# Sparse attention stage of a two-block kernel: values between the turns, masks by pairs, four logit banks, copies by head, gating on GpSimd

## The chip, the cores and the metric

One core of one Trainium2 chip runs the whole kernel. The metric is device time in microseconds (us); lower is better. All times are of one execution of the program.

## What is computed

The kernel computes two transformer-like blocks over 1024 tokens of width 1024. The change lies in the first one's attention. Eight heads of 64 share two key/value heads; each query attends to its causal keys, restricted to the 256 with the highest index score:

```python
logits = einsum('btkgd,btjkd->btkgj', q, k) * 64 ** -0.5
logits = where(selected, logits, -inf)          # causal, top 256 of the index scores
p = softmax(logits, axis=-1)
y_b = einsum('btkgj,btjkd->btkgd', p, v)
merged = concat([rms_norm(y_a, g_out_sgu), rms_norm(y_b, g_out_attn)])
```

y_a is the spatial gating's result, 512 features by 1024 tokens, which is normed in the same stage. merged then goes into the output projection and the rest of the network.

## The kernel before

`attend` is one block of instructions for each engine, between two barriers. Queries are taken in tiles of 128, in the order b = 1, 7, 6, 5, 4, 3, 2, 0; tile b sees b + 1 blocks of 128 keys. A step i is one head u of one tile, 64 steps in all; two steps make a pair p. Tiles with b of 4 and more are called wide here (over 512 keys, two PSUM banks for a head's logits), the others narrow (one bank). Everything is float32.

A step's life: TensorE multiplies queries and keys (`logits`, L1328; two heads of a pair side by side on halves of the rows). VectorE's `mask` (L1494) reads the logits from PSUM and the mask from SBUF, and writes masked logits and their extreme to SBUF. ScalarE's `exponentials` (L1418) works in place. TensorE turns the result with one transpose per block of keys (`turn`, L1342) into PSUM banks 2 and 3; a copy (VectorE L1542, ScalarE L1451) brings each bank to SBUF. After a tile's eight heads, TensorE multiplies with the values (`values`, L1356), in four parts spread over four pairs. The epilogue of a tile follows: ScalarE evicts (L1424), TensorE transposes to tokens (`by_token`, L1365), VectorE divides by the sums (L1501, L1506), ScalarE sums squares (L1430), VectorE makes the mean (L1513), GpSimd the inverse root (L1313), VectorE scales (L1519), TensorE turns back (`turn_y`, L1373), VectorE stores with the gain (L1524). Beside this VectorE selects the keys of the tile after the next steps: `select` has five parts, a count (L1472), a not_equal (L1475), a scan (L1477, L1478), and two closing operations (L1480, L1483), one part per step, the first five steps of a tile.

The order is written out by hand. TensorE runs over pairs p: logits of pair p, the values of an older tile, then both turns of pair p - 1, and at times by_token and turn_y:

```python
if 6 <= p < pairs + 2:
    values((p - 6) // 4, (p - 6) % 4)
if 1 <= p <= pairs:
    turn(2 * p - 2)
    turn(2 * p - 1)
```

VectorE runs over steps i: mask(i), one part of a selection, the copy for step i - 2, epilogue. ScalarE: exponentials(i), the copy for step i - 2, epilogue. Turned banks are numbered n over all steps; VectorE copies the even n, ScalarE the odd: in a wide tile VectorE takes the first half (four blocks) of every head and ScalarE the rest, in a narrow one they take heads in turn. A turn into bank n waits until bank n - 2 is copied. Logits of step i go to banks 4 + 2 (i % 2) and, if wide, the next; they wait until step i - 2 is masked. The exponentials rotate through four SBUF rows.

The norm of the gated part runs beside: GpSimd multiplies its last quarter (L1306), ScalarE squares it, TensorE sums (L1380), ScalarE takes the root by logarithm and exponential (L1435, L1438, at step 8), and VectorE's `norm_gated` (L1531) multiplies four tiles of 128x1024 by gain and root, at steps 42, 44, 46 and 50. PE also runs filler multiplications (`stay_busy`, L174) in the first four pairs.

Of the kernel before, what the change touches and what calls it, by code (L numbers as in the profile page):

```python
# [1229 lines left out]
def attend(nc, K, rot, val, never, found, out, gated):  # L1230
# [9 lines left out]
    GATED = (42, 44, 46, 50)  # L1240
    steps = [(b, u) for b in order for u in range(HEADS)]
    pairs = len(steps) // 2
    banks = [(i, half) for i, (b, _) in enumerate(steps) for half in range(1 if b < 4 else 2)]
    bank_of = {step: n for n, step in enumerate(banks)}
    last_bank = [max(n for n, (of, _) in enumerate(banks) if of == i) for i in range(len(steps))]

    with ExitStack() as ctx:
# [13 lines left out]
        (logits_ready, logits_masked, exp_done, p_turned, p_copied_even, p_copied_odd, pv_ready, y_evicted, y_by_token,  # L1261
         sum_inverted, y_made, y_squared, mean_made, inverted, y_scaled, y_turned, y_stored, power_set) = (K.flag(n).sem for n in (
             "logits_ready", "logits_masked", "exp_done", "p_turned", "p_copied_even", "p_copied_odd", "pv_ready",
             "y_evicted", "y_by_token", "sum_inverted", "y_made", "y_squared", "y_mean_made", "y_inverted", "y_scaled",
             "y_turned", "y_stored", "power_set"))
        psum = K.psum
        p_copied = (p_copied_even, p_copied_odd)
# [9 lines left out]
        def wait_copied(eng, n):  # L1277

            eng.wait_ge(p_copied[n % 2], n // 2 + 1)
# [8 lines left out]
        def copies_of(i, odd):  # L1288

            if not 0 <= i < len(steps):  # L1290
                return []
            return [n for n in range(bank_of[(i, 0)], last_bank[i] + 1) if n % 2 == odd]
# [8 lines left out]
        with nc.Block() as block:  # L1301
            @block.gpsimd
            def _(pool):
# [4 lines left out]
                pool.memset(power[:], -0.5).then_inc(power_set, 1)  # L1308
                pool.wait_ge(power_set, 1)
# [6 lines left out]
            def _(pe):  # L1316
                def logits(p):
# [66 lines left out]
                for p in range(pairs + 5):  # L1384
# [16 lines left out]
                    if 10 <= p <= pairs + 2 and p % 4 == 2:  # L1401
                        by_token((p - 10) // 4)
                    if p == pairs + 2:
                        by_token(NT - 1)
                    if 12 <= p <= pairs + 4 and p % 4 == 0:
                        turn_y((p - 12) // 4)
                    if p == pairs + 4:
                        turn_y(NT - 1)

            @block.scalar  # L1410
            def _(act):
# [28 lines left out]
                for i in range(len(steps) + 8):  # L1440
# [7 lines left out]
                    for n in copies_of(i - 2, 1):  # L1448
                        to, of = turned_bank(n)
                        wait_turned(act, n)  # L1450
                        act.activation(to, of, ACT.Copy).then_inc(p_copied_odd, 1)  # L1451
                    if i >= 20 and i % HEADS == 4:
                        evict(i // HEADS - 2)
                        if i > len(steps):
                            evict(NT - 1)
                    if i >= 21 and i % HEADS == 5:
                        mean_square(i // HEADS - 2)
                        if i > len(steps):
                            mean_square(NT - 1)

            @block.vector
            def _(dve):
# [23 lines left out]
                def mask(i):  # L1486
# [7 lines left out]
                    dve.tensor_tensor_reduce(out=logit[:, i % COPIES, 0:n], in0=keys(LOGITS + 2 * (i % 2), n),  # L1494
# [34 lines left out]
                def norm_gated(t):  # L1529
                    dve.wait_ge(gated_rooted.sem, gated_rooted.n + 2)  # L1530
                    dve.scalar_tensor_tensor(out=gated[:, t, :], in0=gated[:, t, :], scalar=K.col("g_out_sgu", t),  # L1531
                                             in1=gated_root, op0=ALU.mult, op1=ALU.mult).then_inc(gated_normed.sem, 1)

                for i in range(len(steps) + 10):
                    if i < len(steps):
                        mask(i)
                    if i // HEADS < len(SCORED):
                        select(i // HEADS, i % HEADS)
                    for n in copies_of(i - 2, 0):
                        to, of = turned_bank(n)  # L1540
                        wait_turned(dve, n)
                        dve.tensor_copy(to, of).then_inc(p_copied_even, 1)  # L1542
                    if i >= 21 and i % HEADS == 5:
                        divide(i // HEADS - 2)
                        if i > len(steps):
                            divide(NT - 1)
                    if i >= 22 and i % HEADS == 6:
                        mean(i // HEADS - 2)
                        if i > len(steps):
                            mean(NT - 1)  # L1550
                    if i >= 23 and i % HEADS == 7:
                        scale(i // HEADS - 2)
                        if i > len(steps):
                            scale(NT - 1)
# [3497 lines left out]
```

## Time and profile before

| what | value |
|---|---|
| timed runs | 2945.14, 2945.43, 2947.02 us; median 2945.43 |
| span of the profiled execution | 2938.1 us (the median is 7.3 us above it) |
| PE matmul busy in the span | 2820.8 us, 96% |
| VectorE (DVE) | 1898.6 us, 65% |
| ScalarE (ACT) | 1317.8 us, 45% |
| GpSimd (POOL) | 227.2 us, 8% |
| attention stage | from 385.1 us; next stage's first matmul 558.4 us |

The profile comes from one execution of its own; its span is the time from its first to its last instruction. PE is the matmul side of TensorE, PEld its weight loads. Busy time of an engine counts only instructions that compute; PEclk is the clock granted to TensorE as a share of full speed.

### The profile page before, as it was taken

The page shows a single profiled execution, that of the slowest core. Times are in us where ns is not written, and L with a number is a line of the kernel's source. Part 1 is how long each engine was busy: PE and PEld are TensorE (multiplying, and loading weights), DVE is VectorE, ACT ScalarE, POOL GpSimd, SP SyncE. Part 2 cuts the span into 40 slices and gives each one's busy share as a digit, 9 for nine tenths or more (in the row PEclk, how much of TensorE's full clock was granted, in tenths as well). Part 3 has the DMA queues.
Part 4 walks back from the last instruction along what each step waited for, and adds up shares of the span by engine and source line. Part 5 has one row for each costly group of instructions (what it writes and reads, how often), then busy time and mean ns, then how long its engine had stood idle before and what let it go on. Part 6 is the DMA issues. An engine that isn't in the chain of part 4 may idle for free. (4 is left out here: it accounts for less than half of the span.)

```text
span 2938.1 us, 44898 instructions
## 1 busy us (share of the span) xinstructions
PE 2820.8 (96%) x18276; PEld 2228.5 (76%) x18276; DVE 1898.6 (65%) x2882; ACT 1317.8 (45%) x1906; POOL 227.2 (8%) x403
## 2 busy tenths in 40 slices
PE   7999978899999999989999999999899999999998
PEld 4775644577788888867778888887787888888886
DVE  6768977557766466783877524555656576655676
ACT  4027754458555434453441113443324565543344
POOL 0004610001000000000000001110000110000000
PEclk9999999999999999999999999999999999999999
DMA  7520100236666888731463341114324656678884
GB/s 264 172 87 8 51 8 1 93 115 207 225 219 224 306 261 297 253 116 54 133 158 119 125 138 54 53 54 107 147 83 151 208 201 229 225 268 269 289 295 151
DMA packets 195998, 471.32 MB, mean 160 GB/s; under 512 B 31632, under 2 KB 60432, under 8 KB 189456
## 3 DMA queue, kind: packets, MB, share of 16 engines
q1 hardware_dynamic: 178896, 392.94, 40.6%
q0 software_dynamic: 16896, 75.51, 6.4%
q8 instruction: 145, 2.38, 0.3%
q14 instruction: 61, 0.50, 0.1%
HBM read 344.09 MB, written 124.29 MB: 159 GB/s over the span
## 5 line engine op out<-in xcount | busy, mean ns | idle before, releaser
L1991 PE MATMUL psum<-merged_operand 128*128 128x512 f32 x1536 | 360.7, 390 | 0.0
L1991 PEld LDWEIGHTS psum<-merged_operand 128*128 128x128 f32 x1536 | 288.4, 188 | 60.7
L1991 PE MATMUL psum<-h_half_operand 128*128 128x512 f32 x1344 | 316.8, 391 | 0.0
L1991 PEld LDWEIGHTS psum<-h_half_operand 128*128 128x128 f32 x1344 | 252.2, 188 | 55.5 <-issue 1.0
L1991 PE MATMUL psum<-h_half_operand,weight_parts_operand 128*128 128x512 f32 x768 | 177.5, 392 | 0.8 <-DVE weight_parts_operand L2480 0.6
L1991 PEld LDWEIGHTS psum<-h_half_operand,weight_parts_operand 128*128 128x128 f32 x768 | 143.5, 188 | 34.1 <-DVE weight_parts_operand L2480 2.7
L215 DVE CAST weight_high<-weight_ring 128x1024 fp32r<-128x1024 f32 (+1 forms) x64 | 40.0, 625 | 185.8 <-PE psum L3428 105.5
L3428 PE MATMUL psum<-h_high,weight_high 128*128 128x512 f32 x480 | 152.0, 398 | 0.1
L3428 PE MATMUL psum<-h_low,weight_high 128*128 128x512 f32 x480 | 148.1, 390 | 0.0
L3428 PE MATMUL psum<-h_high,weight_low 128*128 128x512 f32 x480 | 147.9, 389 | 0.0
L2480 DVE TENSOR_TENSOR weight_parts_operand<-weight_ring,weight_parts_operand 128x1024 fp32r<-128x1024 f32 x66 | 80.7, 1223 | 85.2 <-ACT weight_parts_operand L2140 84.8
L2480 DVE TENSOR_TENSOR h_half_operand<-hidden_upper,h_half_operand 128x1024 fp32r<-128x1024 f32 (+1 forms) x58 | 74.1, 1297 | 72.3 <-ACT h_half_operand L2275 51.6
L2480 DVE TENSOR_TENSOR h_half_operand<-o,h_half_operand 128x1024 fp32r<-128x1024 f32 (+1 forms) x58 | 74.1, 1297 | 70.9 <-ACT h_half_operand L2275 50.4
L3428 PEld LDWEIGHTS psum<-h_high,weight_high 128*128 128x128 f32 x480 | 89.3, 188 | 27.1 <-issue 9.7
L3428 PEld LDWEIGHTS psum<-h_high,weight_low 128*128 128x128 f32 x480 | 90.1, 188 | 19.1
L3428 PEld LDWEIGHTS psum<-h_low,weight_high 128*128 128x128 f32 x480 | 90.1, 188 | 19.0
L2480 DVE TENSOR_TENSOR merged_operand<-o,merged_operand 128x1024 fp32r<-128x1024 f32 (+1 forms) x50 | 64.3, 1308 | 60.7 <-ACT merged_operand L2275 53.8
L2480 DVE TENSOR_TENSOR merged_operand<-hidden_upper,merged_operand 128x1024 fp32r<-128x1024 f32 (+1 forms) x50 | 64.3, 1308 | 57.7 <-ACT merged_operand L2275 51.3
L2140 ACT ACTIVATE weight_parts_operand<-weight_ring 128x1024 fp32r<-128x1024 f32 x59 | 62.3, 1056 | 84.9 <-PE psum L1962 59.5
L1991 PE MATMUL psum<-x_operand,merged_operand 128*128 128x512 f32 x384 | 93.4, 392 | 1.4 <-issue 1.4
L1991 PE MATMUL psum<-x_operand,h_half_operand 128*128 128x512 f32 x384 | 92.4, 389 | 0.0
L1962 PE MATMUL psum<-h_half_operand,weight_parts_operand 128*128 128x512 f32 x384 | 89.4, 395 | 2.3 <-DVE h_half_operand L2480 2.3
(628 smaller groups left out, 6133.9 us busy)
## 6 DMA issues: line engine op xcount, KB each, us to landing
o<-in_w_ff SPq DMA_DIRECT2D x80, 512.0 KB, 4.6
merged<-hidden_terms SPq DMA_DIRECT2D x56, 512.0 KB, 5.9
hidden_upper<-in_w_ff_down SPq DMA_DIRECT2D x48, 512.0 KB, 4.7
weight_ring<-in_w_out SPq DMA_DIRECT2D x32, 512.0 KB, 3.6
hidden_terms<-weight_parts POOLq DMA_DIRECT2D x16, 1024.0 KB, 7.9
hidden_terms<-weight_ring POOLq DMA_DIRECT2D x16, 1024.0 KB, 7.6
hidden_upper<-in_w_ff_up SPq DMA_DIRECT2D x32, 512.0 KB, 4.4
o<-hidden_terms SPq DMA_DIRECT2D x28, 512.0 KB, 6.2
```

The costliest lines, as they stand in the source:

```text
L215: dve.tensor_copy(high, x).then_inc(sem, 1)
L1962: mm = pe.matmul(mix_bank(i), w[:, at], tiles(h, k), start=(k == 0 and m == 0), stop=(k == KT - 1 and m == 2))
L1991: mm = pe.matmul(bank, w[:, at:at + P], tiles(r, i), start=opens and m == 0, stop=closes and m == 2, skip_group_check=resumed)
L2140: act.activation(w_high(n), K.ring[:, n % RING, :], ACT.Copy).then_inc(w_rounded.sem, 1)
L2480: return dve.tensor_tensor(out=low, in0=of, in1=plain(high), op=ALU.subtract)
L3428: mm = pe.matmul(banks(n)[:, g, :], w[:, n % 2, cols], x[:, k, at(g)], start=(k == 0 and m == 0), stop=(k == KT - 1 and m == 2))
```

## The change

It does six things in the attention stage. (1) TensorE does the first head's turn, then the values, then the second head's turn; values start at pair 5 instead of 6, and the epilogue's steps are one pair or two steps earlier. (2) ScalarE copies all turned banks of even steps, one step after their exponential, VectorE all of odd steps. (3) VectorE masks both heads of a pair at even i, and copies at odd i, ahead of the selection's part. (4) In narrow tiles logits rotate through four banks instead of two. (5) VectorE's four gating operations go; GpSimd multiplies the four tiles by the gain early, and by the root when it is there, before the inverse roots of the epilogue. (6) At the end the epilogue steps of the last two tiles fall in the same iteration, as before, written by `due`.

```diff
-    GATED = (42, 44, 46, 50)
+    EVICT, DIVIDE, SQUARE, MEAN, SCALE, STORE = 18, 19, 19, 20, 21, 23
+    BY_TOKEN, TURN_Y, VALUES_FROM = 9, 11, 5
+    def copier(n):
+        return banks[n][0] % 2
+    copied_by = [sum(copier(m) == copier(n) for m in range(n + 1)) for n in range(len(banks))]
+    def due(at, first, every):
+        a, rest = divmod(at - first, every)
+        if rest or not 0 <= a < NT - 1:
+            return ()
+        return (a, NT - 1) if a == NT - 2 else (a,)
...
-            eng.wait_ge(p_copied[n % 2], n // 2 + 1)
+            eng.wait_ge(p_copied[copier(n)], copied_by[n])
...
-            return [n for n in range(bank_of[(i, 0)], last_bank[i] + 1) if n % 2 == odd]
+            return [n for n in range(bank_of[(i, 0)], last_bank[i] + 1) if copier(n) == who]
+        def logit_banks(i):
+            if i < HEADS:
+                return [LOGITS + 2 * (i % 2)]
+            if steps[i][0] < 4:
+                return [LOGITS + i % 4]
+            return [LOGITS + 2 * (i % 2), LOGITS + 2 * (i % 2) + 1]
+        bank_user, masked_first = {}, []
+        for i in range(len(steps)):
+            masked_first.append(max([bank_user.get(bank, -1) + 1 for bank in logit_banks(i)]))
+            bank_user.update((bank, i) for bank in logit_banks(i))
...
+                for t in range(4):
+                    if t == 3:
+                        pool.wait_ge(gated_squared.sem, gated_squared.n + 1)
+                    pool.tensor_scalar(gated[:, t, :], gated[:, t, :], K.col("g_out_sgu", t), None, op0=ALU.mult) \
+                        .then_inc(gain_taken, 1)
+                pool.wait_ge(gated_rooted.sem, gated_rooted.n + 2)
+                for t in range(4):
+                    pool.wait_ge(gain_taken, t + 1)
+                    pool.tensor_tensor(out=gated[:, t, :], in0=gated[:, t, :], in1=gated_root, op=ALU.mult) \
+                        .then_inc(gated_normed.sem, 1)
...
-                            if lo == 0 and i >= 2:
-                                pe.wait_ge(logits_masked, i - 1)
+                            if lo == 0 and masked_first[i]:
+                                pe.wait_ge(logits_masked, masked_first[i])
-                            mm = pe.matmul(psum[:, LOGITS + 2 * (i % 2) + lo // HALF, 0:w],
+                            mm = pe.matmul(psum[:, logit_banks(i)[lo // HALF], 0:w],
...
-                    if p == 6:
+                    if 1 <= p <= pairs:
+                        turn(2 * p - 2)
+                    if p == VALUES_FROM:
                         pe.wait_ge(gated_rooted.sem, gated_rooted.n + 1)
-                    if 6 <= p < pairs + 2:
-                        values((p - 6) // 4, (p - 6) % 4)
+                    if VALUES_FROM <= p <= pairs:
+                        values((p - VALUES_FROM) // 4, (p - VALUES_FROM) % 4)
                     if p == pairs + 1:
                         for part in range(4):
                             values(NT - 1, part)
                     if 1 <= p <= pairs:
-                        turn(2 * p - 2)
                         turn(2 * p - 1)
...
+                    for a in due(p, BY_TOKEN, 4):
+                        by_token(a)
+                    for a in due(p, TURN_Y, 4):
+                        turn_y(a)
...
-                    for n in copies_of(i - 2, 1):
+                    for n in copies_of(i - 1, 0):
...
+                    for a in due(i, EVICT, HEADS):
+                        evict(a)
+                    for a in due(i, SQUARE, HEADS):
+                        mean_square(a)
...
-                def norm_gated(t):
-                    dve.scalar_tensor_tensor(out=gated[:, t, :], in0=gated[:, t, :], scalar=K.col("g_out_sgu", t),
-                                             in1=gated_root, op0=ALU.mult, op1=ALU.mult).then_inc(gated_normed.sem, 1)
-                    if i < len(steps):
+                    if i < len(steps) and i % 2 == 0:
                         mask(i)
+                        mask(i + 1)
+                    if i % 2:
+                        for n in copies_of(i - 2, 1):
+                            to, of = turned_bank(n)
+                            wait_turned(dve, n)
+                            dve.tensor_copy(to, of).then_inc(copied_by_dve, 1)
                     if i // HEADS < len(SCORED):
                         select(i // HEADS, i % HEADS)
-                    for n in copies_of(i - 2, 0):
-                        to, of = turned_bank(n)
-                        wait_turned(dve, n)
-                        dve.tensor_copy(to, of).then_inc(p_copied_even, 1)
...
-                    if i in GATED:
-                        norm_gated(GATED.index(i))
```

## Rows read from the trace of the kernel before

**Rows 1.** Windows by query tile: length, PE, PEld, DVE, ACT, POOL busy, PEclk, DMA, GB/s.
```profile
385.11:399.75 14.64, 12.13 (x57) 7.38 (x57) 10.48 (x25) 6.86 (x18) 2.53 (x3) 0.88 0.00 1
399.75:425.67 25.92, 20.11 (x90) 10.82 (x89) 19.97 (x33) 17.07 (x28) 0.00 (x0) 0.87 0.00 1
425.67:452.13 26.46, 21.36 (x116) 11.12 (x115) 19.60 (x35) 13.82 (x27) 0.58 (x1) 0.94 0.00 0
452.13:475.38 23.25, 20.35 (x119) 10.85 (x118) 19.03 (x39) 12.35 (x27) 0.56 (x1) 1.00 0.00 1
475.38:497.11 21.73, 18.61 (x111) 9.89 (x110) 17.28 (x38) 10.68 (x27) 0.55 (x1) 1.00 0.00 1
497.11:517.36 20.25, 18.27 (x80) 8.53 (x79) 15.45 (x33) 9.13 (x24) 0.00 (x0) 0.92 0.01 1
517.36:536.73 19.37, 16.85 (x71) 7.50 (x70) 10.61 (x28) 8.17 (x23) 1.52 (x1) 0.91 0.00 1
536.73:549.02 12.29, 11.11 (x59) 5.59 (x58) 6.85 (x31) 6.94 (x27) 1.10 (x2) 1.00 0.00 1
549.02:558.41 9.39, 5.31 (x25) 2.70 (x25) 4.77 (x11) 2.64 (x6) 1.27 (x2) 0.78 0.00 0
```

**Rows 2.** Waits of the whole stage: waiter, releaser, us in total, times, longest.
```profile
ACT q_k_qi_ki L1418 <- DVE minus_max L1494: 70.7, 48, 3.8
PEld psum L1328 <- DVE minus_max L1494: 15.3, 19, 2.4
PE psum L1342 <- DVE p_turned_sbuf L1542: 14.6, 15, 2.2
```

**Rows 3.** Timeline, TensorE, a pair of query tile 5: start, us, operation, idle before.
```profile
464.27 1.56 PE L1328 MATMUL psum<-q_k_qi_ki 64*128 64x512 f32 x8
465.76 1.08 PE L1356 MATMUL psum<-p_turned_sbuf,values 128*64 128x512 f32 x4
466.77 0.88 PE L1342 MATMUL psum<-consts,q_k_qi_ki 128*128 128x128 f32 x6
468.50 0.84 PE L1342 MATMUL psum<-consts,q_k_qi_ki 128*128 128x128 f32 x6 [0.85 <-DVE p_turned_sbuf L1542]
```

**Rows 4.** Timeline, TensorE, a pair of query tile 6.
```profile
446.14 1.77 PE L1328 MATMUL psum<-q_k_qi_ki 64*128 64x512 f32 x8
447.84 1.94 PE L1356 MATMUL psum<-p_turned_sbuf,values 128*64 128x512 f32 x8
449.71 0.98 PE L1342 MATMUL psum<-consts,q_k_qi_ki 128*128 128x128 f32 x7
451.24 0.95 PE L1342 MATMUL psum<-consts,q_k_qi_ki 128*128 128x128 f32 x7 [0.55 <-DVE p_turned_sbuf L1542]
```

**Rows 5.** Timeline, a pair of query tile 3: VectorE's gating and TensorE.
```profile
506.19 1.28 DVE L1531 SCALAR_TENSOR_TENSOR merged<-merged,cols,q_k_qi_ki 128x1024 f32<-128x1024 f32 x1
508.13 0.69 PE L1328 MATMUL psum<-q_k_qi_ki 64*128 64x512 f32 x1 [1.15 <-DVE minus_max L1494]
```

**Rows 6.** Groups by form in the stage; the last, L1030, in the whole kernel.
```profile
L1494 DVE CUSTOM_DVE_ANT_0 q_k_qi_ki<-psum,score 128x1024 f32<-128x1024 f32 x8 | 9.8, 1220 | 5.4 <-PE psum L1328 3.2 <-issue 1.5 <-DVE equal L1475 0.7
L1542 DVE COPY p_turned_sbuf<-psum 128x512 f32<-128x512 f32 x36 | 24.9, 691 | 15.8 <-PE psum L1342 10.6 <-DVE above L1472 2.1 <-issue 1.9
L1451 ACT ACTIVATE p_turned_sbuf<-psum 128x512 f32<-128x512 f32 x12 | 7.0, 579 | 0.1
L1478 DVE TENSOR_TENSOR_SCAN rank<-away,equal 128x1024 f32<-128x1024 f32 x1 | 2.3, 2291 | 0.0
L1306 POOL TENSOR_TENSOR merged<-merged 128x512 f32<-128x512 f32 x2 | 2.5, 1266 | 3.4 <-SPq L1301 3.4
...
L1030 POOL TENSOR_SCALAR marks<-score,test_bits 128x384 f32<-128x384 f32 x22 | 27.4, 1244 | 22.2 <-DVEq L1205 22.2
```

**Rows 7.** GpSimd's timeline at 1753.9 us, and line L4116: ns min/median/max.
```profile
1753.93 1.28 POOL L4252 TENSOR_TENSOR a_off_diagonal<-state_space,chunk_consts 128x512 f32<-128x512 f32 x1 [7.55 <-DVE state_space L4097]
...
L4116 DVE COPY_PREDICATED t<-chunk_consts,a_low x8: 739/747/1184, 1754.6 to 1970.8; 128x512 f32<-128x512 uint32 x8
```

More of the change, by code:

```diff
@@ L1260, in attend @@
         away = K.sbuf(ctx, "away", [P, 1])
-        (logits_ready, logits_masked, exp_done, p_turned, p_copied_even, p_copied_odd, pv_ready, y_evicted, y_by_token,
-         sum_inverted, y_made, y_squared, mean_made, inverted, y_scaled, y_turned, y_stored, power_set) = (K.flag(n).sem for n in (
-             "logits_ready", "logits_masked", "exp_done", "p_turned", "p_copied_even", "p_copied_odd", "pv_ready",
+        (logits_ready, logits_masked, exp_done, p_turned, copied_by_act, copied_by_dve, pv_ready, y_evicted, y_by_token,
+         sum_inverted, y_made, y_squared, mean_made, inverted, y_scaled, y_turned, y_stored, power_set, gain_taken) = (K.flag(n).sem for n in (
+             "logits_ready", "logits_masked", "exp_done", "p_turned", "p_copied_by_act", "p_copied_by_dve", "pv_ready",
              "y_evicted", "y_by_token", "sum_inverted", "y_made", "y_squared", "y_mean_made", "y_inverted", "y_scaled",
-             "y_turned", "y_stored", "power_set"))
+             "y_turned", "y_stored", "power_set", "gated_gain_taken"))
         psum = K.psum
-        p_copied = (p_copied_even, p_copied_odd)
+        p_copied = (copied_by_act, copied_by_dve)
         gated_squares = turned[:, 1].rearrange("p k g j t -> p (k g j t)")[:, 0:S]
@@ L1286, in turned_bank, with copies_of @@
                     psum[:, TURNED + n % 2, 0:width * P].rearrange("p (k t) -> p k t", t=P))
-        def copies_of(i, odd):
+        def copies_of(i, who):
             if not 0 <= i < len(steps):
                 return []
-            return [n for n in range(bank_of[(i, 0)], last_bank[i] + 1) if n % 2 == odd]
+            return [n for n in range(bank_of[(i, 0)], last_bank[i] + 1) if copier(n) == who]
[9 more added lines that the diff above has]
+            bank_user.update((bank, i) for bank in logit_banks(i))
         def wait_turned(eng, n):
@@ L1447, in _ @@
                         root_gated()
-                    for n in copies_of(i - 2, 1):
+                    for n in copies_of(i - 1, 0):
                         to, of = turned_bank(n)
                         wait_turned(act, n)
[L1451 to L1459, printed above, removed]
+                        act.activation(to, of, ACT.Copy).then_inc(copied_by_act, 1)
+                    for a in due(i, EVICT, HEADS):
+                        evict(a)
+                    for a in due(i, SQUARE, HEADS):
+                        mean_square(a)
             @block.vector
@@ L1493, in mask @@
                         dve.wait_ge(p_turned, last_bank[i - COPIES] + 1)
-                    dve.tensor_tensor_reduce(out=logit[:, i % COPIES, 0:n], in0=keys(LOGITS + 2 * (i % 2), n),
+                    dve.tensor_tensor_reduce(out=logit[:, i % COPIES, 0:n], in0=keys(logit_banks(i)[0], n),
                                              in1=never[:, score_at(b):score_at(b + 1)], scale=-HD ** -0.5,
@@ L1543, in _ @@
[L1543 to L1554, printed above, removed]
@@ L1555, in _ @@
-                    if i >= 25 and i % HEADS == 1:
-                        store(i // HEADS - 3)
-                        if i > len(steps) + HEADS:
-                            store(NT - 1)
-                    if i in GATED:
-                        norm_gated(GATED.index(i))
+                    for a in due(i, DIVIDE, HEADS):
+                        divide(a)
+                    for a in due(i, MEAN, HEADS):
+                        mean(a)
+                    for a in due(i, SCALE, HEADS):
+                        scale(a)
@@ L1561, in _ @@
+                    for a in due(i, STORE, HEADS):
+                        store(a)
                 K.dve_done.n = c.n
```

9 lines of the change are left out of this document (removed).

## The prediction

> **What bounds the kernel now.** The profiled execution spans 2938.1 us; the three timed runs have a median of 2945.4 us (2945.1 to 2947.0), so some 7.3 us lie around the span. I make every sum inside the span and subtract it from the median. A difference of about 0.2% (6 us) is what a measurement of this kernel can tell from none.
>
> The change touches the attention stage alone. It begins at 385.1 us and ends at a barrier; after it TensorE resumes at 558.4 us [rows 1]. No DMA moves in it (share 0.00 to 0.01), so what is saved there shifts the rest forward unchanged. I read the stage first by query tile: its 173.3 us hold 144.1 us of busy PE, 124.0 of DVE, 87.7 of ACT, 8.1 of POOL [rows 1]. No engine is full everywhere. The granted clock is 0.88, 0.87 and 0.94 in the first three stretches, 1.00 in the next two, about 0.92 in the next two: part of the PE "busy" there is work at 1.2 GHz instead of 2.4.
>
> Then the waits [rows 2]. ScalarE waits 70.7 us for masks: it has room. PE waits 14.6 us for VectorE's copy of turned values, and 15.3 us (weight loads) for masks. The timeline shows where: in a pair of heads of query tile 5, logits take 464.27 to 465.76, the value products 465.76 to 466.77, the first turn starts at 466.77, and the second only at 468.50, 0.85 us idle, waiting for a copy out of the bank that it reuses [rows 3]. In tile 6 this gap is 0.55 us [rows 4]. In a narrow tile (4 blocks of keys) both turns go in one run, but the logits of a pair have just two banks: VectorE first does a 1.28 us gating scale, then a mask, and only then, after a wait of 1.15 us, PE's second head starts, at 508.13 [rows 5].
>
> **Part by part.** PE's price per piece, from start to next start at full clock: logits of a pair 1.70 us at 7 key blocks and 1.49 at 6, that is 0.21 per block and 0.21 fixed; value products 1.01 for one block of keys, 1.87 for two; one head's turn lasts 0.95 at 7 blocks and 0.84 at 6, less 0.06 that overlaps the next piece: 0.11 per block plus 0.12 [rows 3, 4]. The transposes to and from tokens, of four blocks each, cost like a turn of four, some 0.6; there are two per tile.
>
> 1. *Values between the turns, copies split by head.* The second turn no longer follows the first at once; 1.0 to 1.9 us of value products lie between. ScalarE now copies both banks of an even head: 0.58 us for 512 columns once the first half is turned [rows 6], then the other half, at most as long; VectorE takes 0.69 for the same. It ends 1.9 us after the turn began, and 1.0 (turn) plus 1.0 to 1.9 (values) covers it. VectorE copies both banks of an odd head, and the next logits (1.3 to 1.7 us) cover those. So the gaps of 0.55 to 0.85 us, 16 pairs, close. ScalarE gains 0.1 to 0.3 us a pair in the wide tiles, hidden by its 70.7 us of waits.
>
> 2. *Masks by pairs.* Both masks now run right behind the logits, before any copy or selection. At 7 blocks two take 2.1 us (1.22 each at 8 [rows 6], 0.13 less per block), so they end 4.0 us after the pair's start, and the next logits, at about 5.7, don't wait for them; nor does the first turn for the exponential, which follows its mask. Selection and scaling steps of up to 2 us can still delay a mask; four consecutive pairs average that out. I leave 0.7 us a tile for it.
>
> 3. *Summed for the middle tiles at full clock.* Tile 6 (four pairs): logits 4 x 1.70 = 6.8; turns, two of the tile before and six of its own, 2 x 1.0 + 6 x 0.89 = 7.3; values of 1, 2, 2, 2 blocks 1.0 + 3 x 1.87 = 6.6; token transposes 1.3; total 22.0, with 0.7 is 22.7 against 26.5 [rows 1]. The others in this order of terms. Tile 5: 6.0 + 6.4 + 6.6 + 1.3 = 20.3, so 21.0 against 23.3. Tile 4: 5.1 + 5.6 + 5.8 + 1.3 = 17.8, so 18.5 against 21.7. VectorE needs in tile 6 eight masks (8.4), four copies of both banks (4.4), the next selection at 6 blocks (5.2, of which the scan 1.7) and the epilogue of an earlier tile (2.0): 20.0, in tiles 5 and 4 likewise 17.7 and 15.2. It stays under PE, but by two to three us only. Gain 3.8 + 2.3 + 3.2 = 9.3.
>
> 4. *Four banks for narrow tiles, gating off VectorE.* With one bank per head logits can run a pair ahead of the masks, and 4 x 1.28 = 5.1 us [rows 5] leave VectorE. Tile 3: 4.3 + 4.6 + 4.9 + 1.3 = 15.1, so 15.8 against 20.3 [rows 1]; VectorE's remaining work is 12.4. Tile 2: 3.4 + 3.8 + 4.9 + 1.3 = 13.4, so 14.1 against 19.4. Part of this is clock: with PE dense the 0.92 should be 1.00. Tile 0: bound by the chain mask, exponential, turn; about 10 against 12.3. Gain 4.5 + 5.3 + 2.3 = 12.1.
>
> 5. *The end.* Before, the value products of the last two tiles follow each other after the last copy; now those of the last but one are done an iteration earlier, so the last tile's chain starts one product group (0.9 us) sooner: gain 1.0 of 9.4.
>
> 6. *The beginning without contention.* Tiles 1 and 7 are set by VectorE and by ScalarE's root of the gated sum. The pair order lets mask and exponential of tile 7 start about 1.2 us earlier; ScalarE's copy for head 7 no longer stands behind the root. Tile 7 has about 20.4 us of VectorE work in 25.9. I take 1.2 + 4.3 = 5.5.
>
> 7. *GpSimd's new work.* It does four scalings and four products of 128x1024. A 128x512 product takes 1.27 us on GpSimd, so 2.5; a tensor_scalar of 128x384 took 1.24 us [rows 6], so 3.3 by columns; I take the products' 2.5. All 20 us end near 420 us; GpSimd has nothing to do in the whole second stretch now [rows 1], so on its own queue this is free, and nobody needs the result before the barrier. But VectorE pays. A predicated copy whose operands all lie in SBUF takes 747 ns in the median and 1184, the longest of eight, the one time that a GpSimd product runs beside it, from 1753.93 to 1755.21 [rows 7]. The Trainium skill, "SBUF — State Buffer", section "SBUF: two separate sides", states this as a lock: the pair of ports that VectorE and GpSimd share is held for a whole instruction, and the other blocks fully, where VectorE uses two SBUF inputs or a two-port mode; the rows just named agree with it. The affected VectorE steps are the selections' not_equal, scan and two closing operations, the scan with 2.29 us the longest [rows 6]; masks and copies read PSUM and should pass. In tile 1 GpSimd starts at 387.6 (its two present products from 385.1 on, 1.27 each); walking its ops and VectorE's alternately, the four selection steps each wait 1.5 to 2.2 us for the rest of a 2.5 us operation, and with the 4.2 us that VectorE idles there now (14.64 less 10.48 [rows 1]), tile 7's first mask comes about 3.6 us later than without. In tile 7 the four products start at the root, by this walk near 411; two closing steps wait 2.3 us and less: 2.9. Sum 6.5, bounds 0 and six full waits, 15.
>
> Total: 9.3 + 12.1 + 1.0 + 5.5 - 6.5 = 21.4 us, 2945.4 - 21.4 = 2924.0.
>
> **Rivals.**
> A, *no blocking.* The stretched copy may be peculiar to predicated copies, or the operations fall into gaps. Then 27.9 us are gained: 2917.5. The one stretched copy is thin evidence, and it is of another kind of operation.
>
> B, *VectorE bounds the wide tiles.* Its order is masks, selection, copy of the odd head, selection; the copy has to wait for the second turn, now the last thing in PE's pair, and then one more selection step stands before the next masks. With scan and divide in one pair VectorE has 7.2 us of work against PE's 6. Then the closed gap reappears as logits waiting for masks; tiles 6 to 4 gain 2 instead of 9.3, tile 7 two less: 2933.5. Against it: after the next logits end, the pair has over 1 us of slack in the average pair.
>
> C, *the narrow tiles don't speed up*, because the chain of mask, exponential and turn, not the bank, sets their pace, so that the change does not do what its four banks are for; only the 5.1 us of gating and the last us are gained there: 12.1 becomes 5.5 and the time 2930.5. For it: ScalarE waits most of all for masks [rows 2]; against: the wait of [rows 5] is one for a bank.
>
> D, *slower.* The first turn now stands directly behind the logits; before, 1.0 to 1.9 us of values lay between. If the first head's exponential ended later than the logits, PE would stall, in some 20 pairs by 1.5 us, 30 us against the other gains of 21: 2954. It decides when the exponential ends after the next logits. Against it: ScalarE idles 70.7 us for masks, over 1 us a head [rows 2], so an exponential follows its mask, and the second head's mask moves earlier by a copy and a selection.
>
> E, *nothing*: B and the full 15 us of blocking together, 2942.
>
> **Numbers.** Forecast 0.42, A 0.2, B 0.18, C 0.1, E 0.05, D 0.05. The range takes in A with a clock that stays up (2914) and B with some more blocking (2937). Faster 0.92, same 0.04, slower 0.04.
>
> **What would show it.** The stage shrinks from 173.3 to about 152 us. PE's wait for VectorE's copies (14.6 us) falls under 3. Tile 3 and 2 stretches fall to 16 and 14 us with clock 1.00. Selection steps between 388 and 420 us show durations over 2 us (3.5 for a closing step that takes 1.28 alone); if they keep 1.28, A is right. Mask waits before logits in tiles 6 to 4 growing over 5 us mean B. Idle before first turns, released by exponentials, beyond 10 us in tiles 6 to 2 means D.

## The result, and the profile after

The changed kernel takes 2919.4 us in the median of four runs (2915.9 to 2928.5), the kernel before 2945.7 in the runs beside it: a ratio of 0.9907, 95% interval 0.9889 to 0.9924. A second measurement of five runs gave 0.9920 (0.9906 to 0.9933), 2922.3 us. 2924.0 us was forecast. One execution of the last kernel of the experiments, 2966.9 us at a granted clock of 0.919 where its others had 0.985 to 0.987, is left out below.

The windows of the stage by query tile, with the columns of [rows 1] (length; busy time of PE, PEld, DVE, ACT and POOL; PEclk); tile 1 first, the end last:

```profile
385.25:398.37 13.12, 10.15 (x57) 6.60 (x57) 12.15 (x25) 6.74 (x18) 13.12 (x7) 1.00 0.01 1
398.37:423.73 25.36, 19.43 (x89) 10.55 (x88) 22.26 (x30) 16.81 (x28) 14.14 (x5) 0.87 0.00 0
423.73:445.92 22.19, 22.19 (x128) 11.92 (x127) 20.52 (x39) 15.14 (x31) 0.58 (x1) 1.00 0.01 2
445.92:466.58 20.66, 20.33 (x119) 10.59 (x119) 17.80 (x37) 12.12 (x27) 0.56 (x1) 1.00 0.00 1
466.58:484.66 18.08, 17.74 (x107) 9.40 (x106) 15.56 (x37) 10.48 (x26) 0.55 (x1) 1.00 0.00 0
484.66:500.07 15.41, 15.13 (x79) 6.70 (x78) 13.10 (x35) 9.43 (x26) 0.55 (x1) 1.00 0.00 2
500.07:513.66 13.59, 13.41 (x72) 5.83 (x71) 8.53 (x26) 8.03 (x25) 0.55 (x1) 1.00 0.01 1
513.66:524.83 11.17, 9.80 (x56) 4.53 (x55) 6.45 (x29) 6.46 (x25) 0.55 (x1) 1.00 0.00 1
524.83:533.29 8.46, 4.09 (x21) 2.20 (x21) 3.89 (x11) 2.06 (x6) 1.27 (x2) 0.83 0.00 0
```

The stage is 148.0 us long instead of 173.3, 25.3 us less; 21.4 were forecast. From tile 6 to tile 2 PE is busy for 98% of the time or more (22.19 of 22.19, 20.33 of 20.66, 15.13 of 15.41) and the clock is 1.00, where [rows 1] have 0.94 in tile 6, 0.92 in tile 3 and 0.91 in tile 2. Tile 7 still runs at 0.87, and the end at 0.83.

The waits of the stage, to be read beside [rows 2], and below them one more line of the kernel before, for the fifth of these:

```profile
ACT p_turned_sbuf L1484 <- PE psum L1378: 48.2, 30, 3.3
ACT q_k_qi_ki L1451 <- DVE minus_max L1523: 4.9, 6, 2.6
PEld psum L1364 <- DVE minus_max L1523: 4.0, 6, 1.3
PE psum L1378 <- ACT p_turned_sbuf L1484: 3.9, 2, 3.6
PEld psum L1378 <- ACT q_k_qi_ki L1451: 8.3, 11, 0.8
PE psum L1378 <- DVE p_turned_sbuf L1566: 3.4, 3, 1.5
```

```profile
PEld psum L1342 <- ACT q_k_qi_ki L1418: 13.7, 13, 2.4
```

ScalarE's wait for masks fell from 70.7 to 4.9 us. It now waits 48.2 us for turned values instead, which costs nothing where PE is full. PE's wait for VectorE's copies went from 14.6 to 3.4 us; its three waits of 1.2, 0.8 and 1.5 us all lie in tiles 1 and 7. The first pair of tile 4 on TensorE (the turns in it are still those of tile 5), against [rows 3, 4]:

```profile
466.58 1.35 PE L1364 MATMUL psum<-q_k_qi_ki 64*128 64x512 f32 x8
467.86 0.88 PE L1378 MATMUL psum<-consts,q_k_qi_ki 128*128 128x128 f32 x6
468.67 1.94 PE L1392 MATMUL psum<-p_turned_sbuf,values 128*64 128x512 f32 x8
470.53 0.87 PE L1378 MATMUL psum<-consts,q_k_qi_ki 128*128 128x128 f32 x6
```

Logits, turn, values, turn, with no idle time noted: each piece starts 0.8 to 1.9 us after the one before.

One more thing must be read before two single profiles are compared. The profiled execution of after spans 2927.0 us, only 11.1 less than before's, though its stage is 25.3 shorter. The other 14 us go in parts that the change does not touch. First come three stretches of after, then the same three of before, with the same numbers of matmuls:

```profile
1240.00:1320.00 80.00, 70.83 (x292) 52.20 (x291) 58.38 (x75) 37.11 (x46) 0.00 (x0) 0.89 0.25 89
1900.00:1980.00 80.00, 75.62 (x2086) 68.64 (x2084) 42.28 (x101) 29.12 (x49) 9.15 (x11) 0.98 0.14 49
1980.00:2120.00 140.00, 121.79 (x1029) 104.60 (x1028) 80.92 (x143) 47.13 (x60) 4.57 (x2) 0.90 0.41 134
```

```profile
1265.20:1342.65 77.45, 69.24 (x292) 51.09 (x291) 58.33 (x75) 37.01 (x46) 0.00 (x0) 0.93 0.25 92
1920.50:1997.60 77.10, 74.11 (x2086) 67.13 (x2084) 42.27 (x100) 29.09 (x49) 9.14 (x11) 1.00 0.14 51
1997.60:2131.20 133.60, 117.67 (x1029) 101.68 (x1030) 82.66 (x143) 47.12 (x60) 4.56 (x2) 0.94 0.44 141
```

They take 80.00 us against 77.45, 80.00 against 77.10 and 140.00 against 133.60, together 11.9 of the 14 us, and in each the granted clock is lower in after: 0.89, 0.98, 0.90 against 0.93, 1.00, 0.94. Most of that is a matter of the single execution: 17 runs of the kernel before, later on, lay between 2939.4 and 2956.5 us, nine of the changed one between 2915.9 and 2928.5, and the medians are 22 and 26 us apart in the two measurements, about as the stages are. So the stage's length in the profile is the measure in the experiments below, and medians where a whole time is judged.

### The profile page after: what moved, and what is told of

It reads as the page before. It is cut to its first block and busy times, and to the rows that moved or that the text cites. A ratio compares the mean times of both kernels' runs of the same rounds, so it can differ in the third digit from the quotient of the medians.

```text
span 2927.0 us, 44908 instructions
## 1 busy us (share of the span) xinstructions
PE 2818.4 (96%) x18276; PEld 2229.7 (76%) x18276; DVE 1892.5 (65%) x2878; ACT 1317.8 (45%) x1906; POOL 251.1 (9%) x411
## 3 DMA queue, kind: packets, MB, share of 16 engines
q1 hardware_dynamic: 178896, 392.94, 40.9%
## 5 line engine op out<-in xcount | busy, mean ns | idle before, releaser
L3444 PEld LDWEIGHTS psum<-h_high,weight_high 128*128 128x128 f32 x480 | 89.6, 189 | 28.0 <-issue 10.6
```

The lines of the kernel that those rows point to most:

```text
L3444: mm = pe.matmul(banks(n)[:, g, :], w[:, n % 2, cols], x[:, k, at(g)], start=(k == 0 and m == 0), stop=(k == KT - 1 and m == 2))
```

## Experiments

Each stands against the changed kernel's stage (148.0 us, tiles as above) unless it says otherwise. The stage runs from its first logits to the first filler matmul behind the barrier. Where only one execution of a kernel was timed, its whole time is given for completeness and decides nothing, since runs of one kernel differ by 12 us and more.

### Values ahead of both turns

```diff
-                    if 1 <= p <= pairs:
-                        turn(2 * p - 2)
...
                     if 1 <= p <= pairs:
+                        turn(2 * p - 2)
                         turn(2 * p - 1)
```

> The changed kernel with part 1 undone: values ahead of both turns again, copies still split by head. The stage took 148.1 us in the changed kernel (385.2 to 533.3) and 173.3 before. My account (the second turn is what the order covers): the second turn of a wide pair now waits for both halves' copy on ScalarE, about 1 us in 16 pairs, so the stage is 12 to 20 us longer than in the changed kernel and PE's wait for ScalarE's copies (3.9 us) rises over 10. Rival, the order of the values matters little and the gain came from masks and banks: under 4 us longer.

Measured: stage 159.8 us, 11.8 longer; total 2932.0. Tiles 5 and 4 take 23.36 and 21.11 us, almost what they took before the change. TensorE's timeline in tile 5, and the windows of tiles 5 and 4:

```profile
462.26 1.94 PE L1392 MATMUL psum<-p_turned_sbuf,values 128*64 128x512 f32 x8
464.13 0.87 PE L1378 MATMUL psum<-consts,q_k_qi_ki 128*128 128x128 f32 x6
465.57 0.63 PE L1378 MATMUL psum<-consts,q_k_qi_ki 128*128 128x128 f32 x4 [0.56 <-ACT p_turned_sbuf L1483]
...
448.99:472.35 23.36, 20.49 (x119) 10.58 (x118) 17.92 (x37) 12.21 (x28) 0.56 (x1) 1.00 0.00 1
472.35:493.46 21.11, 17.91 (x107) 9.42 (x106) 15.61 (x37) 10.92 (x28) 0.55 (x1) 1.00 0.00 0
```

The turns follow each other directly and the second waits 0.56 us for ScalarE's copy, as in the other wide pairs; 16 such waits come to 10.6 us, 3.0 of them at ScalarE's root in tile 7. The loss is 2.9, 2.7 and 3.0 us in tiles 6, 5 and 4, 1.4 and 0.6 in tiles 3 and 2, 1.1 in tile 0 and the end together. Of the parts taken away one at a time, the order of turns and values costs the most. The loss is just under what was expected (12 to 20).

### Masks by step

```diff
-                    if i < len(steps) and i % 2 == 0:
+                    if i < len(steps):
                         mask(i)
-                        mask(i + 1)
```

> The changed kernel with VectorE masking one head per step again; copies, banks and turns as changed. My account: the second mask stands behind a part of a selection again, which the slack of a pair (over 1 us) mostly absorbs: the stage is 1 to 5 us longer than 148.1. Rival, masks by pairs carry the gain because logits and exponentials were held by the second mask (ScalarE's wait for masks fell from 70.7 to 4.9 us): over 8 us longer.

Measured: stage 154.5 us, 6.4 longer, between the two expectations; total 2926.6. The window of tile 1:

```profile
383.73:398.46 14.73, 12.01 (x56) 7.86 (x56) 11.28 (x26) 6.43 (x17) 14.73 (x7) 0.88 0.00 1
```

Tile 1 loses 1.6 us, tile 6 1.0, tile 5 0.8, tile 4 0.2, tiles 3 and 2 nothing. Tile 7 came out 2.8 longer, at 28.16 us, but that this is due to the masks is not shown: the kernel with masks by step and two banks, below, runs the same code in this tile in 24.62 us, less than the 25.36 of the changed kernel. Tile 7 also differs by 2.2 us between the changed kernel and the one with two banks (23.20), whose code there is the same; the last section shows what differs. Without tile 7 the loss is 3.6 us, within what was expected.

### Two logit banks in narrow tiles

```diff
-            if i < HEADS:
-                return [LOGITS + 2 * (i % 2)]
             if steps[i][0] < 4:
-                return [LOGITS + i % 4]
+                return [LOGITS + 2 * (i % 2)]
```

> The changed kernel with narrow tiles on two logit banks instead of four. My account: tile 3 took 15.4 us and tile 2 13.6 us in the changed kernel (20.3 and 19.4 before); part of that is the gating that left VectorE. With two banks the masks of a pair must end before the next logits: 2 to 6 us longer in tiles 3, 2 and 0 together. Rival, masks by pairs already free the banks in time: under 1 us.

Windows of tiles 3 and 2:

```profile
482.58:497.99 15.41, 15.13 (x80) 6.70 (x79) 13.10 (x35) 9.41 (x26) 0.55 (x1) 1.00 0.01 2
497.99:511.57 13.58, 13.41 (x71) 5.83 (x71) 8.53 (x26) 8.01 (x24) 0.55 (x1) 1.00 0.00 1
```

15.41 and 13.58 us are what four banks gave (15.41, 13.59), and tile 0 with the end takes 19.64 against 19.63. The rival is right and my account wrong: with masks by pairs and without gating on VectorE the banks are free in time. The total of 2915.0 is one run; its stage is 2.3 us shorter through tile 7, where the code is the same.

### Four banks and nothing else

The kernel before, with the same choice of bank in narrow tiles as the change, and the wait for step i - 4 there:

```diff
-                                pe.wait_ge(logits_masked, i - 1)
+                                pe.wait_ge(logits_masked, masked_before(i))
-                            mm = pe.matmul(psum[:, LOGITS + 2 * (i % 2) + lo // HALF, 0:w],
+                            mm = pe.matmul(psum[:, logit_bank(i) + lo // HALF, 0:w],
```

> The kernel before with four logit banks in narrow tiles and nothing else of the change. My account: while the gating stands on VectorE before masks (tile 3 with 20.24 us and tile 2 with 19.37), a second pair of banks lets TensorE issue logits ahead of it, but the turns then wait for the same late masks: under 2 us of gain in tiles 3, 2 and 0. Rival, the wait for a bank was the cost: over 4 us.

Tiles 3 and 2:

```profile
494.34:511.66 17.32, 14.98 (x79) 6.76 (x78) 15.48 (x33) 8.53 (x23) 0.00 (x0) 1.00 0.01 1
511.66:527.35 15.69, 13.20 (x71) 5.87 (x70) 10.69 (x28) 8.98 (x25) 1.52 (x1) 1.00 0.00 1
```

17.32 and 15.69 us against 20.25 and 19.37 [rows 1], and 20.96 against 21.68 for the rest: 7.3 us gained by four banks alone, with gating still on VectorE. The rival is right again, in the other direction: in the kernel before, the wait for a bank was the cost, and banks are one of two cures for it. Part of the cost was paid in clock. Tiles 3 and 2 of the kernel before each hold a stretch of 3.4 us at 1.2 GHz (509.8 to 513.2 and 520.1 to 523.5 us), which by itself costs some 1.7 us a tile, half of it, an estimate; here both tiles have 1.00. PE's waits for masks ahead of logits, 3.7 us in these two tiles before, are gone too. The whole stage takes 164.5 us, 8.8 less than before; 1.4 of that is tile 1, whose code is the same as before's (13.24 us at clock 1.00 against 14.64 at 0.88) and is no effect of the banks. The total of one run is 2942.7.

### Gating on GpSimd and nothing else

> The kernel before with one part of the change: gating on GpSimd, early. My account: tiles 3 and 2 lose four operations of 1.28 us of VectorE's, which stood before masks on the path, and get 5 to 8 us shorter; tiles 1 and 7 get 2 to 4 us longer through stretched selection steps; the stage is 2 to 5 us shorter than 173.3. Rival: the stretch falls on VectorE's path in full, 5 us, and the stage stays within 1 us.

The kernel before with GpSimd's eight operations of the change and without norm_gated (L1531). Tiles 3 and 2:

```profile
499.62:516.69 17.07, 16.25 (x79) 7.39 (x79) 13.06 (x31) 9.14 (x24) 0.00 (x0) 1.00 0.01 1
516.69:532.08 15.39, 15.22 (x71) 7.07 (x70) 8.39 (x26) 8.17 (x23) 0.55 (x1) 1.00 0.00 0
```

17.07 and 15.39 us, 7.2 less than in [rows 1]; but tiles 1 and 7 are 0.5 and 2.5 longer, and tile 0 with the end 1.2. Stage 170.0, 3.3 shorter than before's; the median 2943.3 us, ratio 0.9986 (0.9973 to 0.9999). The tiles came out as expected in both directions. Banks alone give 6.6 us in tiles 3 and 2, gating alone 7.2, and all of the change together 10.6, of which the order of turns and values accounts for 2.0 (the loss without it): banks and gating are in large part the same gain.

### Two banks and masks by step together

> The changed kernel with two logit banks in narrow tiles and masks by step, both undone. Two banks alone changed nothing in tiles 3, 2 and 0 (15.41, 13.58, 19.64 us as with four), nor did masks by step alone. My account: either one suffices, so that undoing both costs 1 to 4 us in the three tiles together. Rival, neither matters there, since the values between the turns and the gating made the gain: under 0.3 us.

The two edits shown above. Tiles 3 and 2:

```profile
487.80:503.92 16.12, 15.84 (x79) 6.98 (x78) 13.16 (x35) 9.76 (x26) 0.55 (x1) 1.00 0.01 2
503.92:517.99 14.07, 13.90 (x71) 6.12 (x71) 8.50 (x26) 8.12 (x24) 0.55 (x1) 1.00 0.00 1
```

16.12 and 14.07 us, and 20.67 for the rest: 2.2 us more in the three than in the changed kernel, where undoing either alone cost nothing (stage 153.2, total 2925.3). So masks by pairs and four banks stand in for each other in narrow tiles.

### Copies by half

```diff
     def copier(n):
-        return banks[n][0] % 2
+        return n % 2
```

and VectorE copies at every step, ahead of the selection.

> The changed kernel with turned banks numbered over all steps and split between the engines by parity, so that of each wide head one engine takes the first half and the other the second (ScalarE the first this time). My account: with the values between the turns either split is covered, so the stage stays within 2 us of 148.1. Rival, the split by head is needed (VectorE has less to do and one engine's copies are not interleaved with the other's masks): over 5 us longer.

Stage 153.0 us, 5.0 longer, total 2926.7: tile 7 takes 1.6 more, tile 6 2.5, tile 5 0.6, tile 4 0.7, tiles 3 and 2 nothing. That is at the rival's bound and outside my 2 us, though tile 7, as said, moves by as much with the same code. Since ScalarE has the first halves here and VectorE also copies at even steps, the experiment does not separate the split from the place of the copy; that stays open.

### GpSimd beside VectorE: gating back, and gating in the gaps

The first kernel puts norm_gated back on VectorE at steps 42, 44, 46 and 50 and takes the eight operations off GpSimd. It stands ahead of the step's masks there; in the kernel before it stood at the end of the step.

> The changed kernel with the four gating operations back on VectorE at steps 42, 44, 46 and 50, and nothing of them on GpSimd. My account, GpSimd blocks VectorE's two-input steps: the closing steps of the selections return to 1.28 and 1.15 us (5.4 us less VectorE time in tiles 1 and 7), which shortens these tiles by 3 to 5 us; tiles 3 and 2, where VectorE has slack now, get at most 4 us longer, so the stage stays within 3 us of 148.1. Rival, the stretching costs nothing on the path and VectorE's 5.1 us in the narrow tiles do: stage 3 to 5 us longer.

Stage 147.5 us: tiles 1 and 7 take 11.39 and 23.88 instead of 13.12 and 25.36, tile 6 0.2 less, tiles 3 and 2 1.4 and 1.5 more. That is as expected. So GpSimd's work costs 3.4 us in the early tiles in this pair of profiles and saves 2.9 in the narrow ones, and moving the gating was about neutral: the median of four runs is 2922.2 us (ratio 0.9925, 0.9898 to 0.9953). How much of the 2.9 hangs on the place ahead of the masks was not tried. The 1.7 us of tile 1 are firm (13.11 or 13.12 us in the six profiles with masks by pairs and GpSimd's early work, 11.39 or 11.40 in the three without that work); the 1.5 of tile 7 are not, since the kernel with two banks has GpSimd's work and takes 23.20. The second kernel keeps it on GpSimd, but two operations at a time behind step 8k + 6, where VectorE has no selection:

```diff
+                def gate(k):
+                    pool.wait_ge(logits_masked, HEADS * k + 7)
+                    for t in (2 * ((k - 1) % 2), 2 * ((k - 1) % 2) + 1):
...
+                gate(1)
                 for a in range(NT):
...
+                    if a + 2 < 5:
+                        gate(a + 2)
```

> The changed kernel with GpSimd's eight operations moved to the last quarters of tiles 7, 6, 5 and 4, two in each, where no selection step runs. My account: selection steps keep their own durations, and the stage is 3 to 5 us shorter than 148.1, with tile 1 and tile 7 bearing it. Rival, tiles 1 and 7 are bound by ScalarE's root and by TensorE at its lower clock: under 1 us shorter.

Windows of tiles 1 and 7, and GpSimd's groups:

```profile
383.69:395.08 11.39, 9.77 (x56) 6.41 (x56) 10.42 (x25) 6.36 (x17) 2.52 (x3) 1.00 0.01 1
395.08:419.23 24.15, 19.58 (x89) 10.59 (x88) 18.97 (x32) 17.04 (x29) 0.99 (x1) 0.86 0.00 0
...
L1340 POOL TENSOR_SCALAR merged<-merged,cols 128x1024 f32<-128x1024 f32 x4 | 11.3, 2844 | 33.9 <-DVE minus_max L1529 33.9
L1345 POOL TENSOR_TENSOR merged<-merged,q_k_qi_ki 128x1024 f32<-128x1024 f32 x4 | 9.4, 2364 | 3.2 <-DVE minus_max L1529 3.2
```

Stage 144.9 us, 3.2 shorter, nearly all of it in tile 1 (11.39 against 13.12) and tile 7 (24.15 against 25.36). Undisturbed, GpSimd takes 2.84 and 2.36 us an operation. Its median, 2918.3 us of six runs, does not stand clear of the changed kernel's.

### A shift of the end

> The changed kernel with three dependent VectorE memsets of 128x512 at the end of the stage, some 1.3 us more before the barrier. The changed kernel's four runs spread over 12.6 us, and its profiled run gave 14 us of the stage's 25.2 back after 1240 us, at stretches of lower granted clock. My account: those stretches depend on how the program lies against the times at which the clock is granted, so a shift by 1.3 us moves the part after the stage by several us either way, unlike 1.3. Rival, the later part is slower because of the code: it stays as in the changed kernel, and the total is 1.3 us longer.

Three chained memsets of 128x512 on VectorE at the stage's end. The stage takes 150.1 us, 2.1 longer; the four runs took 2921.4 to 2928.8 us, median 2926.5, 4.7 above the 2921.8 that nine runs of the changed kernel give. The part after the stage took 2384.9 us in its profile, against 2393.7 and 2390.1 in two of the changed kernel, so it moves by more than the shift itself. But runs of one kernel spread as much, so a dependence on the position is not shown.

### The changed kernel again, and the root earlier

> The changed kernel once more, unaltered, for its spread. So far its four runs went from 2915.9 to 2928.5 us, and 17 runs of the kernel before from 2939.4 to 2956.5; the stage is 25.3 us shorter in the profiled pair. My account: the part after the stage is the same in both but for the luck of the granted clock, so the medians differ by about 25 us: 2918 to 2923. Rival, the shorter stage makes the later part slower by some 5 us or more on average: 2925 or above.

2922.3 us, within 2918 to 2923; the stage took 148.06 us, against 148.04 in the first profile, though the part after it differed by 3.6.

The last kernel is gating in the gaps with one line moved, the root of the gated sum:

```diff
-                    if i == 8:
+                    if i == 5:
                         root_gated()
```

> The changed kernel with GpSimd's gating in the gaps of tiles 7 to 4, as in the third experiment of that kind, and with ScalarE's root of the gated sum after step 5 instead of step 8. In the changed kernel the root (4.7 us with two table loads) stands between the exponentials of steps 8 and 9, and PE waits 3.6 us there for a copy behind it. My account: at step 5 ScalarE has room, tile 7 loses 2.5 to 4.5 us against 24.2, the stage comes to 141 to 143 us, the total to about 2914. Rival, tile 7 is VectorE's: the stage stays within 1 us of 144.9.

Tile 7:

```profile
398.39:419.31 20.92, 17.24 (x90) 9.86 (x89) 18.55 (x30) 15.90 (x28) 0.78 (x1) 1.00 0.00 0
```

Tile 7 falls from 24.15 to 20.92 us and its clock is 1.00 where it was 0.86; the stage takes 141.85 us, the shortest here. Its three runs took 2912.9 to 2915.9 us, median 2915.7, which is 6.6 below the median of the unaltered kernel's five runs beside it; the ratio to before is 0.9899 (0.9884 to 0.9914).

## Why the prediction was right, and where not

The time, its direction and the main mechanism held: 2919.4 and 2922.3 for 2924.0, stage 148.0 for 151.9. The stage gained 3.9 us more than forecast. By the table, GpSimd's blocking cost 3.1 less, the losses allowed in tiles 6 to 2 were 2.2 too many, and tile 0 gave 1.2 less. Part of the fit is luck, as step 6 shows. By steps of the prediction:

| step | forecast, us | measured, us |
|---|---|---|
| tile 6 | 22.7 | 22.19 |
| tile 5 | 21.0 | 20.66 |
| tile 4 | 18.5 | 18.08 |
| tile 3 | 15.8 | 15.41 |
| tile 2 | 14.1 | 13.59 |
| tile 0 | 10 | 11.17 |
| the end | 8.4 | 8.46 |
| tiles 1 and 7 without GpSimd | 35.1 (40.6 - 5.5) | 35.3 (gating back) |
| GpSimd's blocking | 6.5 | 3.4 |

*Steps 1 to 3* were right to about half a microsecond a tile: pieces from start to start, added up for TensorE, with 0.7 for losses, of which under 0.4 came. Undoing the order returned the gaps. Rival B, that VectorE would bound the wide tiles, is out: PE is busy 20.33 of 20.66 us in tile 5, and the weight loads of logits wait 0.2 us for masks in tiles 6 to 4, where B needed over 5. Of what was to show step 1, PE's wait for VectorE's copies is 3.4 us and not under 3, but none of it is in tiles 6 to 4. That the copies had to be split by head for this is not shown.

*Step 4* had the size right and the reason incomplete. It gave four banks and gating as two causes of one sum. The runs show two cures of one wait: either alone takes 6.6 or 7.2 of the 10.6 us in tiles 3 and 2, and once masks go by pairs and gating is off VectorE, the banks give nothing. What then limits these tiles is TensorE (15.13 busy of 15.41), so that taking one cure away shows less than it gives alone. Two banks with gating on VectorE, in the new order, were not tried. Rival C is out with its reason: four banks alone shortened these tiles, so the chain of mask, exponential and turn did not set their pace. The 5.1 us that step 4 counted for VectorE's gating were 2.9 when measured in the new order. For tile 0 step 4 said 10 us, bound by its chain, and gained 2.3; it came to 11.17, a gain of 1.1, and no run here tells why.

*Step 5* was right, 8.46 for 8.4: the end has one group of value products ahead of its transposes instead of two, and is 0.93 us shorter.

*Step 6*: the sum for the two tiles came out, 35.3 for 35.1, but by luck. The prediction let tile 1 gain 1.2 and tile 7 4.3 without blocking; with gating back they gained 3.2 and 2.0. Of tile 1's 3.2 us, 1.4 goes with the clock: with before's own code the tile took 13.24 us at clock 1.00 in the kernel with four banks alone, against 14.64 at 0.88. Tile 7 could not gain 4.3 because of the root: ScalarE's copy for step 8 stands behind it, and PE waits, with a low clock after. In the changed kernel:

```profile
409.54 1.73 PE L1378 MATMUL psum<-consts,q_k_qi_ki 128*128 128x128 f32 x7 [3.63 <-ACT p_turned_sbuf L1484]
```

The prediction said that the copy for head 7 no longer stands behind the root; true, and the next head's does. Moving the root freed 3.2 us (24.15 to 20.92), the wait and the low clock together.

*Step 7* named the right mechanism and priced it at nearly twice what it costs: 6.5 for 3.4 (1.7 in tile 1, 1.5 in tile 7, 0.2 in tile 6; the 1.5 hang on which engine begins first, as the last section shows). It also took 2.5 us for each of GpSimd's operations; they take 2.84 and 2.36. The same steps in the kernel before, with their mean ns behind the busy time, then selection steps of the changed kernel in the timeline, one of GpSimd's products, and GpSimd's two lines with min/median/max ns:

```profile
L1475 DVE TENSOR_SCALAR equal<-score,found_bits 128x1024 f32<-128x1024 f32 x1 | 0.8, 750 | 0.0
L1480 DVE SCALAR_TENSOR_TENSOR equal<-rank,ties_needed,equal 128x1024 f32<-128x1024 f32 x1 | 1.3, 1281 | 0.0
L1480 DVE SCALAR_TENSOR_TENSOR equal<-rank,ties_needed,equal 128x896 f32<-128x896 f32 x1 | 1.1, 1148 | 0.0
```

```profile
388.08 1.32 DVE L1504 TENSOR_SCALAR equal<-score,found_bits 128x1024 f32<-128x1024 f32 x1
392.98 1.62 DVE L1509 SCALAR_TENSOR_TENSOR equal<-rank,ties_needed,equal 128x1024 f32<-128x1024 f32 x1
395.33 2.09 DVE L1512 SCALAR_TENSOR_TENSOR score<-score,found_bits,equal 128x1024 f32<-128x1024 f32 x1
412.13 2.80 DVE L1509 SCALAR_TENSOR_TENSOR equal<-rank,ties_needed,equal 128x896 f32<-128x896 f32 x1
417.29 3.14 DVE L1512 SCALAR_TENSOR_TENSOR score<-score,found_bits,equal 128x896 f32<-128x896 f32 x1
...
411.64 2.34 POOL L1343 TENSOR_TENSOR merged<-merged,q_k_qi_ki 128x1024 f32<-128x1024 f32 x1
...
L1338 POOL TENSOR_SCALAR merged<-merged,cols x4: 2841/2846/4677, 387.7 to 398.1; 128x1024 f32<-128x1024 f32 x4
L1343 POOL TENSOR_TENSOR merged<-merged,q_k_qi_ki x4: 2341/2789/3801, 407.9 to 417.1; 128x1024 f32<-128x1024 f32 x4
```

The walk had four steps in tile 1 wait 1.5 to 2.2 us each. They were stretched by 0.57, 0, 0.34 and 0.81 (0.75 to 1.32, the scan not at all, its length is that of [rows 6], 1.28 to 1.62 and to 2.09); in tile 7 the two closing steps were stretched by 1.65 and 1.99 (1.15 to 2.80 and 3.14). The scan had begun first and GpSimd waited: its second tensor_scalar takes 4677 ns instead of 2846. The masks and copies, which read PSUM, passed as the prediction said: a mask of 128x1024 beside GpSimd's product took 1.22 us, as in [rows 6]. Rival A (no blocking) is out: with the operations in the gaps the stage gets 3.2 us shorter. The test set for it, selection steps over 2 us, holds for three of the four closing steps, at most 3.14.

*Rivals D and E* did not happen. No weight load of a turn waited longer than 0.8 us for an exponential (11 waits, 8.3 us in the whole stage, against 13.7 before), where D needed over 10 us in tiles 6 to 2.

One premise was wrong without harm: the 7.3 us between span and median do not lie around the span. In every run here the time is only 1.5 or 1.6 us above its span; the profiled execution of the kernel before was one of the shorter ones.

## What to carry to other kernels

Where an engine waits on a copy between two of its own pieces, put an independent piece between them, and add up its pieces from start to start: where the engine was full, that sum was the new time of the tile. When several edits attack one wait (more buffers, earlier release, less work ahead of the releaser), test each alone and each taken away: here banks or gating alone brought most of the gain, and banks or masks taken away alone cost nothing in the same tiles. Compare the changed stretch and not the whole span when single executions of one kernel differ by more than the part at stake.

## What was not expected of the hardware

GpSimd's two kinds of operation hold VectorE up differently. GpSimd's tensor_tensor has two SBUF operands and takes 2.36 us alone. Beside it VectorE's scalar_tensor_tensor started at 412.13 and ended at 414.93; GpSimd's product, begun at 411.64, ended at 413.98, so VectorE's step ended 0.95 us later, nearly its own 1.15: it waited for the product in full. In turn a product of GpSimd took 3.80 us behind VectorE's scan. Beside GpSimd's tensor_scalar (2.84 us) the same operation of VectorE took 1.62 and 2.09 instead of 1.28 and ended before GpSimd did, and VectorE's tensor_scalar of 128x1024 ran in 1.32 instead of 0.75 us. The Trainium skill, "SBUF — State Buffer", section "SBUF: two separate sides", says that one side fully blocks; the trace agrees for GpSimd's tensor_tensor, and for its tensor_scalar behind VectorE's scan, which it waited for; it does not agree for VectorE's steps begun beside a tensor_scalar, which were stretched by 0.34 to 0.81 us and not held to its end.

Which side waits is decided by tenths of a microsecond. In the kernel with two banks, whose code in tile 7 is the same, the first closing step began at 411.71, before GpSimd's product (411.85), and GpSimd waited; the second met only the end of a product:

```profile
411.71 1.14 DVE L1507 SCALAR_TENSOR_TENSOR equal<-rank,ties_needed,equal 128x896 f32<-128x896 f32 x1
416.87 1.48 DVE L1510 SCALAR_TENSOR_TENSOR score<-score,found_bits,equal 128x896 f32<-128x896 f32 x1
```

1.14 and 1.48 us stand against 2.80 and 3.14, and tile 7 took 23.20 us against 25.36. The clock there was 0.93 against 0.87, but it was 0.93 too in the kernel with the memsets, where VectorE's step began second (411.22, GpSimd's product 411.11), took 3.19 us, and tile 7 came to 25.38. So of these three profiles the order goes with the 2.2 us, and the clock does not.

And one kernel's runs differ by 12.6 (nine runs) and 17.1 us (seventeen) with no change of code; in the pair of profiles above the difference went with time at 1.2 GHz in stages whose code is the same: 67.1 us behind the stage in after and 40.9 in before, and half of these 26.2 us is 13.1 of the 14.0. What made the clock fall there is not shown.
